# One transformer block with 32 experts on one core: the half output projection split by token tile, the first expert gathered directly transposed, the second norm's weights applied at the transposes, small loads moved

## The reference

```python
h = rms_norm(x, norm1_gain)
proj = einsum('bsd,dn->bsn', h, w_in)          # q, k, v of attention, indexer, retention, gate
mixed = concatenate([out_a, out_b], -1)        # out_a: sparse attention, 512 wide; out_b: gated retention, 512
x = x + einsum('bsm,md->bsd', mixed, w_out)
h2 = rms_norm(x, norm2_gain)
logits = h2 @ w_router + b_router              # 32 experts, top 4, softmax over them
for e in range(32):                            # every expert, its tokens weighted by `combine`
    z = h2 @ w1[e] + b1[e]                     # 1024 x 2048
    act = clamped_swiglu(z)
    out = out + combine[..., e:e+1] * (act @ w2[e] + b2[e])   # 1024 x 1024
return rms_norm(x + out, final_gain)
```

## Time and profile before

| | |
|---|---|
| median of 3 runs | 1101.18 us (1098.81 to 1102.26) |
| profiled execution | 1099.66 us, span of its instructions 1097.9 us |
| PE busy | 1047.8 us, 95% |
| DVE, ACT, POOL busy | 290.1, 175.2, 21.0 us |
| moved | 430.14 MB, mean 392 GB/s |
| mean granted clock of TensorE | 0.976 |

### The profile page before, as it was taken

One profiled execution on the slowest core, in us unless ns is written; L12 is line 12 of the kernel. 1 busy time (PEld: TensorE's weight loads), 2 busy tenths in 40 slices (PEclk: granted clock), 3 DMA queues, 4 the chain that ended last, 5 costly groups with the idle time before them and its releaser, 6 DMA issues.

```text
span 1097.9 us, 11722 instructions
## 1 busy us (share of the span) xinstructions
PE 1047.8 (95%) x4652; PEld 402.2 (37%) x4652; DVE 290.1 (26%) x710; ACT 175.2 (16%) x310; POOL 21.0 (2%) x27
## 2 busy tenths in 40 slices
PE   8999899999999999899998989998999898999995
PEld 7458354333333333233332323332333333333331
DVE  2565634222121212121211212121313122211222
ACT  1231322111111111111111111111111111011112
POOL 1202000000000000000000000000000000000000
PEclk9999998999999999999999989998999999999998
DMA  9787816999999999999999999999999999999993
GB/s 331 189 301 285 364 39 267 398 435 426 432 427 435 430 431 431 429 433 426 433 429 432 429 435 425 430 430 432 430 432 436 427 432 429 435 427 433 423 427 157
DMA packets 34135, 430.14 MB, mean 392 GB/s; under 512 B 5068, under 2 KB 6496, under 8 KB 16032
## 3 DMA queue, kind: packets, MB, share of 16 engines
q1 hardware_dynamic: 32256, 426.44, 92.2%
q10 hardware_dynamic: 1216, 1.70, 1.1%
q0 software_dynamic: 640, 1.69, 0.5%
HBM read 427.19 MB, written 2.62 MB: 391 GB/s over the span
## 4 chain that ended last, share of the span: by engine, by line
PE 72%; DMA 25%; DVE 1%; ACT 1%; SPq 1%; issue 0%; DVEq 0%; ACTq 0%
PE ps L1226 30%; DMA w1r<-w_mlp 22%; PE ps L1257 14%; PE ps L1273 6%; PE ps L991 4%; PE ps L1196 3%; PE ps L979 3%; DMA w2r<-w_mlp 2%; PE ps L1113 1%; PE ps L1038 1%; PE ps L1144 1%; PE ps L1204 1%; PE ps L1234 1%; PE ps L1103 1%; DMA w1r<-w_in 1%; PE ps L1281 1%
## 5 line engine op out<-in xcount | busy, mean ns | idle before, releaser
L1226 PE MATMUL ps<-w1r,arena 128*64 128x512 f32 x2048 | 489.9, 614 | 24.3 <-DMA w1r<-w_mlp 24.3
L1226 PEld LDWEIGHTS ps<-w1r,arena 128*64 128x64 f32 x2048 | 140.1, 140 | 292.9 <-issue 259.7
L1257 PE MATMUL ps<-w2r,arena 128*64 128x512 f32 x992 | 218.6, 592 | 3.9 <-DMA w2r<-w_mlp 3.9
L1257 PEld LDWEIGHTS ps<-w2r,arena 128*64 128x64 f32 x992 | 71.1, 137 | 140.0 <-issue 130.6
L901 DVE TENSOR_TENSOR acc<-ps,acc 128x512 f32<-128x512 f32 x64 | 41.2, 686 | 230.4 <-PE ps L1273 230.4
L893 DVE TENSOR_TENSOR arena<-arena 128x512 f32<-128x512 f32 x32 | 22.1, 692 | 172.8 <-ACT arena L548 172.8
L557 ACT ACTIVATE arena<-ps 64x512 f32<-64x512 f32 x32 | 18.9, 592 | 296.4 <-PE ps L1257 296.4
L857 DVE TENSOR_SCALAR sel_z<-small 96x64 bf16 (+1 forms) x32 | 6.1, 191 | 225.6 <-PE ps L1226 225.6
L1273 PE MATMUL ps<-arena 128*128 128x512 f32 x128 | 63.2, 617 | 1.3 <-ACT arena L559 1.3
L1196 PE MATMUL ps<-h,arena 128*64 128x512 f32 x248 | 58.5, 592 | 0.0
L871 DVE TENSOR_SCALAR arena<-small,rank,gate 128x64 f32<-128x64 f32 x128 | 31.3, 307 | 62.9 <-PE ps L1281 62.9
(11 more groups left out here) (230 smaller groups left out, 574.6 us busy)
## 6 DMA issues: line engine op xcount, KB each, us to landing
w1r<-w_mlp SPq DMA_DIRECT2D x54, 4096.0 KB, 31.6
w2r<-w_mlp SPq DMA_DIRECT2D x62, 2048.0 KB, 19.6
w1r<-w_mlp SPq DMA_DIRECT2D x19, 2048.0 KB, 11.7
w1r<-w_in SPq DMA_DIRECT2D x7, 2048.0 KB, 18.5
w1r<-w_mlp SPq DMA_DIRECT2D x6, 1024.0 KB, 6.8
w1r<-w_out SPq DMA_DIRECT2D x2, 2048.0 KB, 13.7
rel_table<-arena ACTq DMA_DIRECT2D x1, 1536.0 KB
acc<-x SPq DMA_DIRECT2D x2, 512.0 KB, 4.4
```

Of the source, the lines that this page charges most:

```text
L1226: ins = mm(ps[64 * c:64 * c + 64, 2 * par + n, :], hgT[:, par, k % 4, 64 * (k // 4):64 * (k // 4) + 64], w1r[:, 8 * par + k, at:at + 512], ...
L1257: ins = mm(ps[at:at + 64, 4 + c, :], actT[:, k % 4, 64 * (k // 4):64 * (k // 4) + 64], (w1r if last else w2r)[:, k // 2, col:col + 512], s ...
```

## The change

- **Half projection**: the wait for `va_sb` moves from both tiles to tile 1.
- **First expert**: its gather multiplies h2 blocks (as weights, 128 columns) with `onehotP` (64 columns) and so writes the transposed input straight into bank 7; there is no `hg`, no transposes for expert 0. Its bias matmuls stand ahead of the gather. The two matmuls that count the sweeps, and DVE's count, come later.
- **Norm weights**: h2 is now x2 without the gain, copied by ACT (`copy_half`). The gain is applied when the transposed input leaves bank 7, by DVE (`take_hgT`) in place of ACT's copy, for all experts. `gain_q` and eight columns of `cols` hold it.
- **Loads**: before, ones and wr move from w1r to the arena; g2b is gone. br and gain_q are loaded by POOL once chunk 1 of w_in is there; before and ones are loaded once the indexer is done; wr after the transposes of the probabilities, and DVE scales it ahead of its first residual. A memset writes the ones of the row sum. Of expert 1, pair 5 is loaded after the half projection, pair 7 (now whole) after the last value product, pair 4 after the last projection.
- **Banks**: x2's transposes use banks 4 and 5 for both tiles; the routings use banks 6 and 3, the ranks bank 6.

```diff
 # SP
             load_win(3)
-            sp.dma_start(before, c_rank[:, 0:P]).then_inc(late_in, 16)
-            sp.dma_start(ones, c_rank[:, P:2 * P]).then_inc(late_in, 16)
-            sp.dma_start(wr, w_router[0].rearrange("(k p) e -> p k e", p=P)).then_inc(late_in, 16)
-            sp.dma_start(g2b, norm2_gain.to_broadcast((P, D))).then_inc(late_in, 16)
-            sp.dma_start(br[:, :], b_router.to_broadcast((P, NE))).then_inc(late_in, 16)
             for c in range(4, 7):
                 load_win(c)
+            sp.wait_ge(idx_added, AH)
+            sp.dma_start(before, c_rank[:, 0:P]).then_inc(rank_in, 16)
+            sp.dma_start(ones, c_rank[:, P:2 * P]).then_inc(rank_in, 16)
...
             sp.wait_ge(proj_done, 8)
             load_w1(0, 2, 2)
+            sp.wait_ge(half_mm, 1)
+            load_w1(1, 1, 5)
+            sp.wait_ge(p_tr, AH)
+            sp.dma_start(wr, w_router[0].rearrange("(k p) e -> p k e", p=P)).then_inc(wr_in, 16)
             sp.wait_ge(pv_done, 4)
-            sp.dma_start(w1r[:, 14, :], w1_v[1, 1, 1, :, 0:2048]).then_inc(w1_first, 16)
+            load_w1(1, 3, 7)
             sp.wait_ge(out_mm, 4)
             load_w1(1, 0, 4)
-            load_w1(1, 1, 5)
-            sp.wait_ge(count_mm, 1)
-            sp.wait_ge(h2_ready, 4)
-            sp.dma_start(w1r[:, 15, :], w1_v[1, 1, 1, :, 2048:4096]).then_inc(w1_in[7], 16)
 # POOL
+            pool.wait_ge(win_in[C_QKB], 16)
+            pool.dma_start(br[:, :], b_router.to_broadcast((P, NE))).then_inc(br_in, 16)
+            pool.dma_start(gain_q, norm2_gain[0].rearrange("(c q j) -> q c j", c=2, q=P)).then_inc(gq_in, 16)
 # ACT
+            def copy_half(t, c):
+                nc.scalar.activation(h2[:, t, :].rearrange("p (j c q) -> p c j q", j=4, c=2)[:, c],
+                                     acc[:, t, 512 * c:512 * c + 512].rearrange("p (q j) -> p j q", j=4), ACT.Copy).then_inc(h2_ready, 1)
...
-            def take_hg(base, e, par):
-                act.wait_ge(gathered, base + e + 1)
+            def take_hg(base, e):
+                act.wait_ge(gathered, base + e)
                 nc.scalar.activation(hg, ps[:, 6, :], ACT.Copy).then_inc(hg_sb, 1)
-                act.wait_ge(hg_tr, base + e + 1)
-                nc.scalar.activation(hgT[:, par], ps[:, 7, :].rearrange("p (c n) -> p c n", c=4), ACT.Copy).then_inc(hgT_sb, 1)
 # DVE
+            def take_hgT(base, e, par):
+                dve.wait_ge(hg_tr, base + e + 1)
+                v.tensor_tensor(hgT[:, par].rearrange("p j (c n) -> p (j c) n", c=2), ps[:, 7, :].rearrange("p (b n) -> p b n", b=8),
+                                cols[:, GQ:GQ + 8].rearrange("p (b a) -> p b a", a=1).to_broadcast((P, 8, SLOTS)),
+                                ALU.mult).then_inc(hgT_sb, 1)
 # TensorE
             pe.wait_ge(wout_in, 32)
-            pe.wait_ge(va_sb, 2)
             for t in range(TT):
+                if t == 1:
+                    pe.wait_ge(va_sb, 2)
                 for c in range(2):
...
-            def gather_first(t):
+            def gather_first(t, blocks):
                 pe.wait_ge(first_pick, t + 1)
                 pe.wait_ge(h2_ready, 2 * t + 2)
-                for c in range(2):
-                    ins = mm(ps[64 * c:64 * c + 64, 6, :], onehotP[:, 0, t, :],
-                             h2[:, t, :].rearrange("p (j c q) -> p c j q", j=4, c=2)[:, c], start=(t == 0), stop=(t == TT - 1))
+                for b in blocks:
+                    ins = mm(ps[:, 7, SLOTS * b:SLOTS * b + SLOTS], h2[:, t, P * b:P * b + P], onehotP[:, 0, t, :],
+                             start=(t == 0 and b == 0), stop=(t == TT - 1 and b == 7))
```

More of the change, by code:

```diff
@@ L142, in hybrid_block @@
         va = carve(high, 5632, [TT, 512])
-        g2b = carve(high, 6656, [D])
-        before, ones = carve(high, 7680, [P]), carve(high, 7808, [P])
-        wr = carve(high, 7936, [KD, NE])
         mixT = carve(arena, 0, [KD, S])
@@ L162, in hybrid_block @@
         top8, top4 = carve(arena, 5408, [TT, 8]), carve(arena, 5424, [TT, TOPK])
-        x2n = carve(arena, 4096, [1024])
+        x2n = carve(arena, 4096, [512])
+        wr = carve(arena, 4608, [KD, NE])
+        before, ones = carve(arena, 5456, [P]), carve(arena, 5584, [P])
+        gain_q = carve(arena, 5780, [2, 4])
         onehotP = carve(arena, 0, [2, TT, SLOTS])
@@ L211, in hybrid_block @@
         w1_in = [sem(f"w1_in{i}") for i in range(8)]
+        w2_in = [sem(f"w2_in{i}") for i in range(2)]
         w1_half = [sem(f"w1_half{i}") for i in range(4)]
-        w1_first = sem("w1_first")
-        w2_in = [sem(f"w2_in{i}") for i in range(2)]
         w1_early = sem("w1_early")
@@ L578, in step, with sweep @@
                     take_y(base, e - 1, 1 - par)
-            def sweep(base, hb):
-                take_hg(base, 0, 0)
+            def sweep(base, hb, start=False):
+                if not start:
+                    take_hg(base, 0)
                 step(base, hb, 0, 0, first=True)
@@ L591, in sweep @@
                 take_y(base, NE - 1, 1)
-            sweep(0, 0)
+            sweep(0, 0, start=True)
             act.wait_ge(sweeps_ready, 1)
@@ L697, in _ @@
             v.tensor_tensor(bsrc[64:96, :], bsrc[32:64, :], bias3[32:64, :], ALU.subtract).then_inc(bias_left, 1)
-            dve.wait_ge(late_in, 80)
-            v.tensor_tensor(wr, wr, cols[:, G2:G2 + KD].rearrange("p (k a) -> p k a", a=1).to_broadcast((P, KD, NE)),
-                            ALU.mult).then_inc(wr_ready, 1)
+            for e in range(2):
+                ins = v.tensor_scalar(sel_z[:, e, :], pick[0:96, e:e + 1].to_broadcast((96, SLOTS)), 1.0, None, ALU.mult)
+            ins.then_inc(sel_first, 1)
             for t in range(TT):
@@ L911, in step @@
                     add_back(hb, m - 1, 0)
+                if not (last and par == 1):
+                    take_hgT(base, e + 1, 1 - par)
+                if par == 1 and not first:
                     add_back(hb, m - 1, 1)
@@ L920, in sweep @@
             def sweep(base, hb, start=False):
-                one_hot(base, 0, 0, free=False)
                 if start:
                     gates()
+                    dve.wait_ge(gq_sb, 1)
+                else:
+                    one_hot(base, 0, 0, free=False)
+                take_hgT(base, 0, 0)
+                step(base, hb, 0, 0, first=True)
+                if start:
                     count_sweeps()
                 gated_one_hot(base, hb, 0, 0, 0, free=False)
-                step(base, hb, 0, 0, first=True)
                 step(base, hb, 0, 1, first=True)
@@ L1051, in _ @@
             pe.wait_ge(diag_ready, 1)
-            pe.wait_ge(late_in, 80)
-            mm(ps[:, 6, 0:S], ones, diag.rearrange("p t n -> p (t n)"), start=True, stop=True).then_inc(row_mm, 1)
+            mm(ps[:, 6, 0:S], ones_early, diag.rearrange("p t n -> p (t n)"), start=True, stop=True).then_inc(row_mm, 1)
             pe.wait_ge(qkb_sb, 2)
@@ L1205, in gather_T @@
                 ins.then_inc(hg_tr, 1)
-            def z_bias(base, e, par, free=True):
-                if free:
-                    pe.wait_ge(z_read, base + e - 1)
-                for n in range(2):
-                    for c in range(2):
-                        at = 1024 * c + 512 * n
-                        mm(ps[64 * c:64 * c + 64, 2 * par + n, :], sel_z[:, par, :], bias3[:, at:at + 512], start=True, stop=False)
             def z_rows(base, lap, k, par, halves, early=None):
@@ L1277, in gates_T @@
                 pe.wait_ge(gated_ready, base + 2 * j + 2)
-                pe.wait_ge(hg_sb, base + (NE if isinstance(j, int) and j == NE // 2 - 1 else 2 * j + 3))
+                pe.wait_ge(hg_sb, base + (NE - 1 if isinstance(j, int) and j == NE // 2 - 1 else 2 * j + 2))
                 for which in range(2):
@@ L1292, in step @@
                 pe.wait_ge(hgT_sb, base + e + 1)
-                if first and par == 1:
-                    pe.wait_ge(w1_first, 16)
-                z_bias(base, e, par, free=not first)
+                if not (first and par == 0 and isinstance(base, int)):
+                    z_bias(base, e, par, free=not first)
                 z_rows(base, lap, 0, par, halves, early=rb + 1 if isinstance(m, int) and (m, par) == (1, 0) else None)
```

91 lines of the change are left out of this document (53 added, 38 removed).

## The result

| | before | changed kernel |
|---|---|---|
| median of the runs beside each other | 1100.91 us (6 runs, 1098.81 to 1102.26) | 1092.38 us (6 runs, 1089.70 to 1094.99) |
| ratio, 95% interval | | 0.9922 [0.9907, 0.9936] |
| the profiled execution | 1099.66, span 1097.9 | 1094.80, span 1092.9 |
| the changed kernel again, profiled at another time | 1100.64 (15 runs) | 1094.67 (10 runs, 1088.28 to 1097.74), ratio 0.9946 [0.9925, 0.9966] |

The forecast was 1091.5 with a range of 1087.5 to 1096.5. The change is faster, by 6 to 8.5 us. But its own 16 runs are spread over 9.5 us, where all runs of the kernel before are spread over 6.9, and their median is 1094.25. Why they lie so wide was a question for the experiments. The second profile of the same kernel answers part of it, so both are shown here: the first (1094.80, an execution from the upper half) and the second (1090.18, span 1088.3).

The account below looks back on a forecast made before the run. From 200 us the DMA engines' stream of expert weights bounds the kernel, so only gains before it count: 5.3 + 4.0 = 9.3 off 1099.66 gives 1090.4, plus 1.0 toward the runs' median, forecast 1091.5 us, range 1087.5 to 1096.5.

Parts of the forecast that it names:

- The claim that one issue sets the end: SP queue's first load waiting for expert 0's fourth used w1 row (w1_used 4, 191.95 us) opens the stream and sets the end.
- microsecond for microsecond: Whatever brings the issue at w1_used 4 earlier ends the kernel earlier by the same amount.
- Part 1: Half projection by token tile: 3.4 us of standstill gone plus 1.9 from full clock, 5.3 us; bounds 3.4 and 5.3.
- The wait for w_out: Ahead of the half projection: its second load lands at 125.9 and still costs 0.1 us.
- Part 2: Small loads and expert 1's w1 pairs moved to other places: worth 0, with bounds 0 and 3.1 us late.
- The margin: w_router's load and DVE's multiply ahead of its first residual: hidden by some 2 us.
- Part 3: From the last projection to expert 0: 4.0 us taken, between 1.1 (clock falls) and 5.8 (full clock).
- the clock falls as before: Rival: low clock again between routing and first row blocks, gain 5.3 + 1.1 = 6.4 us, 1094.3; chance 0.24.
- The page on the clock: Routing stretch: transposes don't count as busy, so matmuls replacing them would keep the clock up; spoke for 1089.6, chance 0.22.
- Part 4: Expert loop: the copy of transposed input passes from ACT to DVE, 31 times 0.68 us, hidden; worth 0.
- The rival of the early gain given back: w_router or w_out lands late, or the clock falls in the half projection: 1094.6, two of them 1096.5; chance 0.10.
- 8 to 10 us: Whole kernel: the forecast's own row of gain, given as 1090.5 to 1093, chance 0.38.

Follow-up runs that it names:

- warm_late: The kernel of warm with expert 1's gather and transposes moved behind the sixth and seventh row block of expert 0; 1091.23 us, ratio 0.9921.
- va_only: The kernel before with one edit: the half projection waits for va only ahead of its second token tile; 1096.65 us, ratio 0.9962.
- va_undone: The changed kernel with the wait for va put back ahead of both token tiles of the half projection; 1098.81 us, ratio 0.9978.
- warm: The changed kernel plus twelve matmuls that nothing reads (fillers), six ahead of the second tile's router matmuls and six behind; 1091.32 us, ratio 0.9918.
- warm_old: The kernel of warm with expert 0 gathered in rows, copied by ScalarE and transposed, as before the change; 1093.19 us, ratio 0.9937.
- old_gather: The changed kernel with expert 0 gathered in rows, copied by ScalarE and transposed, as before the change; 1094.46 us, ratio 0.994.
- take_pieces: The changed kernel with VectorE's scaling of the transposed rows written as eight instructions in place of one, each expert; 1093.35 us, ratio 0.9926.

## Why the prediction was right, point by point

**The claim that one issue sets the end** held: 10 us earlier in the second profile, 9.6 off the span; a delay of 5.15 us in front gave 4.7 in the span, and one of the same size in the stream nothing that could be measured. Its words "microsecond for microsecond" went too far: warm_late's issue came 2.26 us earlier and the span became 0.2 shorter.

**Part 1, 5.3 forecast.** By the first profile: the earlier trace rows's 3.54 us of waiting are gone to 0.04, and 15.67 became 14.00, not 13.73. That is 3.5 and 1.7, 5.2. By medians 4.5 (va_only). The wait for w_out, 0.1 forecast, was 0.04 to 0.33 in the profiles. In the stretch of the half projection the clock was 1.00 where TensorE had not stood and 0.89 behind the 3.54 us.

**Part 2, 0 forecast.** The pair went out behind the half projection, w_router at 145.76 (forecast about 145 to 147), and it landed 2.8 us later, not after 11.3. DVE waited 0.86 us for it and then still stood 2.60 us before its first residual, at 151.65. The margin was forecast as some 2 us. Rows of the first profile:

```profile
148.62 0.43 DVE L822 TENSOR_TENSOR arena<-arena,cols 128x256 f32<-128x256 f32 x1 [0.86 <-DMA arena<-w_router]
...
151.65 0.69 DVE L788 TENSOR_TENSOR acc<-ps,acc 128x512 f32<-128x512 f32 x1 [2.60 <-PE ps L1165]
```

The prediction set beside this the Trainium skill's figure of 512 B a piece for full rate ("DMA: Bandwidth & Descriptors", Specifications). Here 128 KB in pieces of 128 B landed in 2.8 us behind a pair and delayed nothing. What larger pieces would have given no run here shows.

No run takes the loads alone. Something ahead of the half projection did differ: TensorE came to it at 125.80 in the kernel before, at 126.55 in the first profile and at 125.94 in the second, of which 0.4 and 0.05 are a longer wait for the first chunk of w_in. With this the sums close: 5.2 + 0.7 - 0.75 is 5.15 in the first profile, where the issue moved by 5.13, and 5.0 + 5.2 - 0.15 is 10.05 in the second, where it moved by 9.99. Whether the new place of the small loads or chance makes the difference is open, with one profile of the kernel before.

**Part 3, 4.0 forecast between 1.1 and 5.8.** Both ends are what the executions do. Second profile: from the end of the half projection (126.20 + 14.0) to the first row block 32.9 us, where before had 36.3, 3.4 of the 3.8 forecast; from there to the issue 8.84 where before had 10.62, 1.8 of the 2.0. Together 5.2 of 5.8. First profile: 35.5 and 10.69, together 0.7 of the 1.1. The forecast of 4.0 described neither profile; it came near the first median, 1092.38, because the changed kernel mixes both, and the mixture in six runs was partly luck. By the runs part 3 is worth 2.3 us (va_undone against before) and 4.3 or 2.4 (the changed kernel's six and all 16 runs against va_only). This is the part of the sum that was mis-sized, and the second set of runs, 1094.67, is nearer the rival "the clock falls as before" (1094.3) than the forecast. The 14 gathers took 3.32 us at full clock, 3.0 forecast, and 5.92 at the low one. The ACT copies took 1.06 us each and not 0.60:

```profile
166.45 2.12 ACT L524 ACTIVATE h<-acc 128x512 f32<-128x512 f32 x2
```

The last exp ended at 170.98, where the forecast had at worst 176.3 - 5.3 = 171.0; the ranks were done at 170.27, and the gates ended at 171.5, with the gathers running to 175.3: covered. The reason given for part 3, copy, transposes and second copy of ACT out of the way, was for the most part wrong. At full clock the direct gather gives 0.5 to 1.0 us (warm against warm_old, the second profile against old_gather); the rest is left to the order.

**The page on the clock.** By the Trainium skill, "TensorE: Matmul & The Clock Gate", Part 4: PE-mode transpose, transposes do not count as busy for the clock as matmuls do, and the prediction drew from it that matmuls in their place would keep the clock up. In four of seven profiles it fell in gathers made of matmuls alone, in the first to 0.50 from 169.64 to 176.13 us; and warm_old, with four transposes there and fillers ahead, had its row blocks at full clock (3.65 us). The rule, if it acts, doesn't decide this place.

**Part 4, 0 forecast**, held even at 30 us more of VectorE (take_pieces).

**Two slips of the sum.** The rival of the early gain given back adds up to 1094.5 and 1096.4, not 1094.6 and 1096.5. The row "8 to 10 us" faster than 1101.18 is 1091.2 to 1093.2, not 1090.5 to 1093. Neither changes the range.

**The profiled executions** were 1099.66 and 1094.80: 4.9 us apart, where medians lie 8.5 or 6.0 apart. One pair of profiles would have undersold the change, the second pair (9.5) oversold it.

## What to carry to other kernels

Where a kernel fills its buffers and then streams, find the first load that must wait for a used buffer and price every edit ahead of it by the moment of that issue; a delay put on either side of it shows whether that is so. Pulling the issue forward by pushing work behind it gains only until the next issue in the queue waits for that work. If a stretch can run at either clock, its two prices are the forecast and a value between them describes no execution: forecast the mixture, and take many runs: here six and ten of the same kernel gave medians 2.3 us apart.

## What was not expected of the hardware

- The granted clock fell in the same code in some executions and not in others: 28 records of 64 columns took 3.32 us or 5.81 to 6.21; the first chunk's stretch had 1.00 or 0.66 to 0.71; the last down projection took 7.04 or 8.73.
- 14 float32 matmuls of 64 columns with 128 by 128 weights took 3.32 us by the timeline at full clock, 0.237 each. Eight of 32 columns took 1.87 by the same view in before, 0.234 each (0.214 by the chain): half the columns, about the same time.
- ScalarE's copy of 128 by 512 within SBUF, its input read in steps of four elements (L524), took 1.06 us; a plain one out of a bank took 0.60, and ScalarE's square of such a tile, read in order (L513), 0.62:

```profile
165.44 0.62 ACT L513 ACTIVATE arena<-acc 128x512 f32<-128x512 f32 x1
```
